# Tile-by-tile layer norms and moved products behind the experts of a two-block transformer kernel

## The reference, cut to what matters

```python
"""end of the first block: y is the experts' sum"""
x = layer_norm(ALPHA1 * x + g2 * y, post2_g, post2_b)
for i in range(2):                       # second_block
    if i == 0: mix = pool_mixer(x)       # window means per group, 4 products of 256x256, bias, scale
    else:      mix = gated_deltanet(x)   # z = x @ w_z; qkv = silu(conv4(x @ w_qkv)); ba; chunked delta rule;
                                         # o = rms(o) * norm_w * silu(z); o @ w_out
    x  = layer_norm(ALPHA2 * x + mix, ln_gain[i, 0], ln_bias[i, 0])
    ff = square(relu(x @ mlp_w1[i])) @ mlp_w2[i]                       # 1024 -> 4096 -> 1024
    pe = sigmoid(x @ ple_gate_w[i] + ple_gate_b[i]) * (p[i] @ ple_proj[i])
    x  = layer_norm(ALPHA2 * x + ff + pe, ln_gain[i, 1], ln_bias[i, 1])
```

## Time and profile before

| | us |
|---|---|
| three runs | 2159.33, 2158.49, 2153.45 (median 2158.49) |
| profiled execution, device time | 2157.81 |
| its span | 2156.1 |
| TensorE busy in the span | 1956.4 |
| experts (first to last of their products) | about 350 to 1390 |
| mean granted TensorE clock | 0.972 |

### The profile page before, as it was taken

How to read it: one execution, slowest core, us unless ns; L and a number is a source line. 1 busy time by engine, 2 the same in 40 slices (tenths; PEclk the granted TensorE clock), 3 DMA queues, 4 the chain that set the end, 5 groups by cost and what they waited for, 6 DMA issues and landing times. The chain is left out here.

```text
span 2156.1 us, 28523 instructions
## 1 busy us (share of the span) xinstructions
PE 1956.4 (91%) x10917; PEld 1229.7 (57%) x10918; DVE 914.4 (42%) x1463; ACT 456.6 (21%) x525; POOL 68.4 (3%) x123
## 2 busy tenths in 40 slices
PE   4999896999998989999988999779997898889997
PEld 2759764433333334333333343369986887868986
DVE  3799544111111111111111111366545887875554
ACT  2223101000000000000000000124532443324541
POOL 2000002000000000000000000000000000020000
PEclk9999997999999999999999999989999999999999
DMA  9694834959999999899999786464554420054551
GB/s 360 235 329 138 300 137 176 406 211 422 422 422 422 421 423 421 337 422 422 421 422 421 323 375 282 187 207 160 176 199 154 154 99 1 2 182 147 194 188 67
DMA packets 143588, 581.37 MB, mean 270 GB/s; under 512 B 10504, under 2 KB 12536, under 8 KB 94265
## 3 DMA queue, kind: packets, MB, share of 16 engines
q1 hardware_dynamic: 135824, 563.12, 67.1%
q0 software_dynamic: 3040, 11.02, 1.6%
q10 hardware_dynamic: 4649, 6.17, 0.8%
HBM read 579.23 MB, written 1.05 MB: 269 GB/s over the span
## 5 line engine op out<-in xcount | busy, mean ns | idle before, releaser
L1153 PE MATMUL bank<-ring,area 128*64 128x512 f32 x2048 | 461.4, 599 | 28.5 <-DMA ring<-in_w_gu 27.9
L1153 PEld LDWEIGHTS bank<-ring,area 128*64 128x64 f32 x2048 | 144.4, 137 | 327.6 <-issue 236.7
L895 PE MATMUL bank<-area_r,ring_r 128*128 128x256 f32 x992 | 284.6, 287 | 9.5 <-DVE area_r L2029 7.1
L897 PE MATMUL bank<-area_r,ring_r 128*128 128x256 f32 x992 | 282.9, 285 | 0.0
L898 PE MATMUL bank<-area_r,ring_r 128*128 128x256 f32 x992 | 282.8, 285 | 0.0
L288 DVE TENSOR_TENSOR ring_r<-ring,ring_r 128x2048 fp32r<-128x2048 f32 x90 | 206.1, 2292 | 176.6 <-ACT ring_r L285 176.1
L2297 DVE TENSOR_SCALAR area<-bank 128x512 f32<-128x512 f32 x36 | 24.9, 692 | 542.5 <-PE bank L1153 542.5
L285 ACT ACTIVATE ring_r<-ring 128x2048 fp32r<-128x2048 f32 x92 | 175.9, 1913 | 207.5 <-PE bank L898 188.8
L895 PEld LDWEIGHTS bank<-area_r,ring_r 128*128 128x128 f32 x992 | 192.8, 194 | 12.1 <-DVE area_r L2029 7.3
L1191 PE MATMUL bank<-area 128*64 128x512 f32 x864 | 192.5, 594 | 0.5 <-DVE area L2311 0.5
L897 PEld LDWEIGHTS bank<-area_r,ring_r 128*128 128x128 f32 x992 | 192.7, 194 | 0.5 <-issue 0.5
(11 more groups left out here) (331 smaller groups left out, 2048.5 us busy)
## 6 DMA issues: line engine op xcount, KB each, us to landing
ring<-in_w_gu SPq DMA_DIRECT2D x256, 1024.0 KB, 21.2
area<-in_w_dn SPq DMA_DIRECT2D x96, 1024.0 KB, 21.5
ring<-in_mlp_w SPq DMA_DIRECT2D x64, 1024.0 KB, 5.4
ring<-in_w_dn SPq DMA_DIRECT2D x32, 1024.0 KB, 19.9
ring<-in_w_in SPq DMA_DIRECT2D x24, 1024.0 KB, 6.2
ring<-in_gdn_w_in SPq DMA_DIRECT2D x16, 1024.0 KB, 5.5
area<-in_w_mod SPq DMA_DIRECT2D x12, 1024.0 KB, 8.8
ring<-in_w_mod SPq DMA_DIRECT2D x8, 1024.0 KB, 17.2
```

Source lines behind the costliest of these rows:

```text
L895: ins = mm(out_, a_[0], b_[0], start=start, stop=False)
L897: mm(out_, a_[0], b_[1], start=False, stop=False)
L1153: ins = mm(bk[hf * BLK:(hf + 1) * BLK, :], x(kt), block_u[:, c:c + BANK], start=False, stop=kt == ND - 1)
```

## The change

- **Norms by tile.** `layer_norm` behind the experts becomes `tile_norm(t)`; tile 0 is normalised, transposed (`tile_features`) and multiplied (`tile_part`) before tile 1. `tile_part` issues the eight products of a unit's slices with x's high part first and waits for the low part only then. Each part of the gate runs for three units on tile 0, then on tile 1, then unit 3 on both. `copy_high`, `x_low` and `residual` take a tile. The last quarter of w2 is ordered by tile. The last norm's tiles are written out one by one.
- **Projection moved.** `p @ ple_proj` and the transposes of p stand behind the experts and behind gdn_out (`p_product`); ScalarE keeps the result in SBUF (`ple`). Block 0's p and w_proj are loaded by SP before the late stream.
- **GpSimd** multiplies x by ALPHA1 during the experts, adds the experts' banks times g2, scales the pooling weights and bias, loads them earlier, gives one root per tile, and splits low parts of gate units 1 and 2 (both blocks) and of z0's second unit (`unit_low_here`).
- **z and silu.** z's first half goes ahead of qkv in the stream, in the groups and on TensorE; silu of slab s-1 goes ahead of the copies of slab s.

```diff
...
+                add_slab("z0", gdn_in, 3 * C)
                 add("qkv", slabs(gdn_in, range(0, 3 * C)))
-                add("z", slabs(gdn_in, range(3 * C, 4 * C)))
+                add_slab("z1", gdn_in, 3 * C + 1)
...
+        group("pT_0", 1)
+        group("proj_0", 4)
         group("pooled", 4)
         group("pool_tok", 4)
         for i in range(2):
             if i == 1:
                 group("x4T", 4)
+                group("z0", 2)
...
-                group("z0", 2)
...
+                group("pT_1", 1)
+                group("proj_1", 4)
             group(f"xT_{i}", 4)
-            group(f"pT_{i}", 1)
             group(f"gate_{i}", 4)
-            group(f"proj_{i}", 4)
...
+            sp.wait_ge(w_used, PRE + NU * (NE - 1))
+            sp.dma_start(p_tok[0], A["p_2"][0, 0].rearrange("(t p) c -> p t c", p=P)).then_inc(ple_in, 16)
+            sp.dma_start(ple_proj[0], A["ple_proj_2"][0].rearrange("(k p) n -> p k n", p=P)).then_inc(ple_in, 16)
             for n in range(PRE, len(stream)):
                 load(n)
-            sp.wait_ge(x_ready, 5 * NT)
-            sp.dma_start(out[0].rearrange("(t p) d -> p t d", p=P), x_tok).then_inc(out_done, 16)
-            sp.wait_ge(out_done, 16)
+            for t in range(NT):
+                sp.wait_ge(x_ready, 4 * NT + t + 1)
+                sp.dma_start(out[0, t * P:(t + 1) * P, :], x_tok[:, t, :]).then_inc(out_done, 16)
+            sp.wait_ge(out_done, 16 * NT)
...
+            pool.wait_ge(xn_ready, 3 * NT)
+            link(nc.gpsimd.tensor_scalar(x_tok, x_tok, ALPHA1, None, ALU.mult))
+
+            def tile_root(t):
+                inverse_root(rstd[:, t:t + 1])
+
+            def unit_low_here(i):
+                pool.wait_ge(w_high, i + 1)
+                pool.wait_ge(w_split, i)
+                nc.gpsimd.tensor_tensor(unit_low(i), ring[:, i % RING2, :, :], unit_high(i), ALU.subtract)\
+                    .then_inc(w_split, 1)
+
+            full(pool, G("moe", 3))
+            pw = a(6).rearrange("p (g k d) -> p g k d", g=4, k=2)
+            for dst, src in ((pool_b_bc, A["pool_b_2"][0].rearrange("(o g) d -> o (g d)", o=1).to_broadcast([P, D])),
+                             (pool_scale_bc, A["pool_scale_2"][0:1, :].to_broadcast([P, D])),
+                             (pw, A["pool_w_2"][0].rearrange("g (k p) d -> p g k d", p=P))):
+                pool.dma_start(dst, src).then_inc(pool_loads, 16)
+            ytmp = tok(4)
+            for t in range(NT):
+                for hf in range(NH):
+                    cs = slice(hf * BANK, (hf + 1) * BANK)
+                    emptied(pool, G("moe", 2 * t + hf))
+                    nc.gpsimd.tensor_tensor(x_tok[:, t, cs], x_tok[:, t, cs], ytmp[:, t, cs], ALU.add)\
+                        .then_inc(moe_added, 1)
+            tile_root(0)
+            pool.wait_ge(pool_loads, 48)
+            link(nc.gpsimd.tensor_tensor(pool_b_bc, pool_b_bc, pool_scale_bc, ALU.mult))
+            nc.gpsimd.sem_inc(scaled, 1)
+            tile_root(1)
+            for k in range(2):
+                nc.gpsimd.tensor_tensor(pw[:, :, k, :], pw[:, :, k, :], pool_scale_bc.rearrange("p (g d) -> p g d", g=4),
+                                        ALU.mult).then_inc(scaled, 1)
+            load_norm(3)
+            unit_low_here(LATE["gate0"] + 1)
+            tile_root(0)
+            unit_low_here(LATE["gate0"] + 2)
+            tile_root(1)
...
-            norm_root()

...
-            norm_root()
+            tile_root(0)
+            unit_low_here(LATE["z0"] + 1)
+            tile_root(1)
...
+                unit_low_here(LATE["gdn_out"] + i)
             inverse_root(s_["sso"][:, 1, :])
-            norm_root()
+            tile_root(0)
+            unit_low_here(LATE["gate1"] + 1)
+            unit_low_here(LATE["gate1"] + 2)
+            tile_root(1)
...
+            def p_product(i):
+
+                pe.wait_ge(ple_in, 32 * (i + 1))
+                transposed(G(f"pT_{i}"), [(p_tok[i][:, t, m * P:(m + 1) * P], m * S + t * P)
+                                          for m in range(2) for t in range(NT)])
+                emptied(pe, G(f"pT_{i}"))
+                pT = p_T[i].rearrange("p (m t) -> p m t", m=2)
+                for s in range(NH):
+                    for t in range(NT):
+                        g = G(f"proj_{i}", NT * s + t)
+                        claim(pe, g)
+                        for k in range(2):
+                            ins = mm(bank(g)[:, :], pT[:, k, t * P:(t + 1) * P],
+                                     ple_proj[i][:, k, s * BANK:(s + 1) * BANK], start=k == 0, stop=k == 1)
+                        fills(ins, g)
+
+            p_product(0)
...
-            for hf in range(NH):
-                for t in range(NT):
+            for t in range(NT):
+                for hf in range(NH):
...
+            def tile_features(gname, t, done):
+
+                pe.wait_ge(x_ready, done + t + 1)
+                for hf in range(NH):
+                    transposed(G(gname, NH * t + hf),
+                               [(x_tok[:, t, (4 * hf + m) * P:(4 * hf + m + 1) * P], m * P) for m in range(4)])
+
+            def tile_part(name, g, gname, highs, h, t):
+
+                u = late_unit(LATE[name] + h)
+                hf = h % 2
+                if hf == 0:
+                    claim(pe, g)
+                pe.wait_ge(x_high, highs + NH * t + hf + 1)
+                for k in range(UK):
+                    high = parts_of(xs, UK * hf + k, slice(t * P, (t + 1) * P))[0]
+                    for j in range(2):
+                        ins = mm(bank(g)[:, :], high, u[j][:, k, :], start=hf == 0 and k == 0 and j == 0, stop=False)
+                        settle(ins)
+                emptied(pe, G(gname, NH * t + hf))
+                for k in range(UK):
+                    low = parts_of(xs, UK * hf + k, slice(t * P, (t + 1) * P))[1]
+                    ins = mm(bank(g)[:, :], low, u[0][:, k, :], start=False, stop=hf == 1 and k == UK - 1)
+                if hf == 1:
+                    fills(ins, g)
+                    if t == NT - 1:
+                        owed[0] = True
+                elif t == NT - 1:
+                    ins.then_inc(w_used, 1)
+
             def ffn(i):
-                to_features(f"xT_{i}", x_tok, x_ready, NT * (1 + 2 * i))
...
+                def gate_part(n_unit, t):
+                    tile_part(f"gate{i}", G(f"gate_{i}", NT * (n_unit // 2) + t), f"xT_{i}", 12 * i, n_unit, t)
+
+                for t in range(NT):
+                    tile_features(f"xT_{i}", t, NT * (1 + 2 * i))
+                    for n_unit in range(SPLITS):
+                        gate_part(n_unit, t)
+                for t in range(NT):
+                    gate_part(SPLITS, t)
...
-                    for c in range(C):
+                    for c, t in (((0, 0), (0, 1), (1, 0), (1, 1)) if kq < KQ - 1 else ((0, 0), (1, 0), (0, 1), (1, 1))):
                         u = late_unit(n0 + C * kq + c)
...
+                        g = G(f"w2_{i}", NT * c + t)
...
                         if kq == KQ - 1:
-                            owed[0] = True
+                            fills(ins, g)
+                            owed[0] = t == NT - 1
+                        elif t == NT - 1:
+                            ins.then_inc(w_used, 1)
...
-            to_features("x4T", x_tok, x_ready, NT * 2)
-            for q in range(4):
-                emptied(pe, G("x4T", q))
+            for t in range(NT):
+                tile_features("x4T", t, NT * 2)
+                for h in range(2):
+                    tile_part("z0", G("z0", t), "x4T", 4, h, t)
...
-            for h in range(2):
-                z_half(0, h)
...
+            p_product(1)
...
+            p_columns(0)
             late.below(2)
+            p_products(0)
+            late.below(3)
...
+            def copy_high(gname, t):
+
+                for hf in range(NH):
...
+                    f(feat_r(X_HIGH)[:, 4 * hf:4 * hf + 4, t * P:(t + 1) * P],
+                      bank(g)[:, :].rearrange("p (m c) -> p m c", c=P), ACT.Copy).then_inc(x_high, 1)
...
+                late.below(w0 + 3)
+                for t in range(NT):
+                    copy_high(f"xT_{i}", t)
...
-            copy_high("x4T")
+            copy_high("x4T", 0)
+            late.below(LATE["qkv"] + 1)
+            copy_high("x4T", 1)
...
+            late.below(w0 + 3)
+            silu_z(0)
             for s in range(6):
                 late.below(w0 + 2 * s + 4)
-                if s >= 2:
-                    act.wait_ge(conv4_ready, s - 1)
+                if s:
+                    silu(s - 1)
...
-                if s:
-                    silu(s - 1)
-                late.below(w0 + 2 * s + 5)
+                if s < 5:
+                    late.below(w0 + 2 * s + 5)
             silu(5)
-            late.below(w0 + 16)
...
-            load_ffn(1)
```

(67 more changed lines are left out.)

167 lines of the change are left out of this document (61 added, 106 removed).

## The result

The changed kernel took 2135.6 us (median of four runs, 2132.9 to 2138.5) against 2156.2 for the kernel before beside it: ratio 0.990, 95% interval 0.988 to 0.992. Four further runs of it gave 0.988 (0.985 to 0.990). The forecast was 2117 us, with a range of 2104 to 2138: the direction and the range held, but the gain is 20.6 us where 41.5 were forecast. The profiled execution took 2138.45 us (span 2136.7), at the upper edge of the four.

A forecast was written before the change was run, and what follows sets the result against it. The prediction took TensorE, busy 91% of the span, as the bound, leaving its idle time, slow clock and the end to win. Its terms 20 + 20 + 1 + 4 - 3 = 42 took 2158.5 to about 2117 us, range 2104 to 2138.

The forecast's parts named there:

- A: From the experts' last product to w1 of block 0: earlier pooling and gate by tile save 20 us.
- The term for GpSimd beside VectorE, -3: Of 35 us new GpSimd work, some 4 lie beside VectorE passes of two SBUF tensors: 3 us lost, bounds 0 and -28.
- Rival 1: Contention in full: each VectorE pass under a long GpSimd instruction is held, norms late at A and B; 2141, chance 0.10.
- ALPHA1, costed at nothing: GpSimd's multiply of x by ALPHA1 has the whole expert loop to hide in: no cost.
- its own sign: Account of A is wrong if block 0's gate starts after 1424; its first product was forecast near 1418.
- B: From the end of block 0's w2 to the first k transposes: 123.8 us become 103.6, 20 saved, TensorE waiting 6.
- C: From gdn_out's end (F) to block 1's w1: queue order and banks collide, 5.9 us wait, gate at F+19.1; saves 1.
- Rival 2: No bank collision in C, or ScalarE passes pT sooner: gate at F+11.7, 8 us more, 2109; chance 0.12.
- D: The end: tile 0 finished and sent before products end, tile 1 done 4.6 us after them instead of 8.0; saves 4.
- Rivals 3 to 5: Qkv slabs VectorE-bound, 2127, chance 0.13; gate and z0 products at half clock, 2171, 0.03; edits ineffective, 2158, 0.02.

The follow-up runs named there:

- the run with all pieces: Changed kernel with GpSimd's long instructions cut to 512 columns, ALPHA1 multiply behind the routing, ScalarE's order and projection banks behind gdn_out changed: 2115.0 us, ratio 0.981.
- The bench: Changed kernel whole, with 27 pairs of GpSimd and VectorE operations timed beside each other on idle memory behind its end: 2221.6 us.

## Why the prediction was right and wrong

- **A, forecast 20, measured 6.5.** The adds were priced right (1.24 us each for 1.25), and the order of events is that of the text. The times were not. The gate starts 13 us later than forecast, counted from the experts' end. Along the path VectorE and GpSimd lose to each other 0.9 (first pass), 1.0 and 0.9 (roots, 1.56 and 1.47 for 0.56), 0.8 (the bias), 2.0 (tile 1's second pass), 3.0 (L2491) and 4.1 us (tile 0's second pass), together 12.7. They are not all on one path, and w1 starts 14.4 us later than forecast. Pieces win back 6.9. No run takes GpSimd out of A altogether: in the run with all pieces A is still 7.5 us over the forecast, and its stretched rows add up to some 6. So for that half the hold is read from rows and not shown by an edit.
- **The term for GpSimd beside VectorE, -3, is the step that failed.** "Some 4 us of it lies beside such passes": the sum counted how long the two overlap, where it had to count the rest of GpSimd's instruction at each pass that comes up under it. The 35 us were the right amount of work; in place of the 3, the rows show 12.7 (A), 4.1 (C) and 0 to 6 in the routing. Rival 1 had the mechanism and, at 2141, nearly the time. It was given 0.10, with L2521 counted for it and, against it, that reads with a PSUM side are not stretched and that most of the 35 us fall where VectorE has slack. The first of these is true and no argument, since the norm passes have no PSUM side; the second failed at the passes named above. L2521's 0.6 us are the same rule: it came up 0.7 us before the end of the splits. One row with a short overlap can't tell a hold from a proportion.
- The Trainium skill states the rule outright (SBUF — State Buffer, on the two sides of the memory): the pair of ports is an exclusive lock, taken for the whole instruction by whichever comes first, against VectorE instructions in a two-port mode or with two SBUF inputs, the latter only against a GpSimd instruction that reads SBUF. The bench agrees in all cases but one, the memset's too: beside the one-tensor multiply, operations of two tensors are let go 3.5 us after its start and not at its end at 5.36, and there the measurement decides. The forecast cited another page of it, which speaks of contention only, and weighed that as a rate.
- **ALPHA1, costed at nothing: wrong.** "The whole loop to hide in" asked whether GpSimd has time, not who is working when it starts. It cost about 3 us in the profile.
- **B, forecast 20, measured 19.7: right**, with its 6 us wait and the vanished ones. Its parts were off: the text gave z0 about 5 us for itself, where all but silu gives 12.3 alone and 9.1 on top of silu, and the new wait is partly slack. That the hold cost nothing here was luck: two passes missed GpSimd's split by a fraction of a us, and the forecast had not looked at that.
- **C, forecast 1, measured -3.5.** Collision, order, 5.9 us wait and the gate's start (F+19.6 for F+19.1) are confirmed to half a us once the hold is gone, and C then takes 43.0 for 43.6 before; the hold adds the rest. Rival 2 did not come, as the text had argued.
- **D, forecast 4, measured 4.0: right.** Rivals 3 to 5 did not come: the slabs run without waits at 12.4 us, the gate's stretch in A had a mean clock of 0.90 (its first products alone slow), and the gain is there.
- **The rest** is in front: 7.4 us. The routing alone took 7.5 longer, some 3 of them the hold and 4.6 the clock of the router.

The range held because it was drawn nearly to rival 1's 2141, not because the forecast was near. Half of the forecast gain is missing, and by its own sign (the gate's start) the account of A was wrong.

## What to carry to other kernels

Before giving elementwise work to GpSimd, list what VectorE does while it runs. Charge each elementwise operation that touches only SBUF with the rest of GpSimd's instruction, whatever its own length; operations with a PSUM operand and the norm's statistics went free here. Keep such instructions on GpSimd short (the bench's 512-column subtraction lets VectorE begin 1.1 us after its start) or start them where VectorE has long waits. With a queue order written by hand, ask of each new first item what stands behind it: two lines swapped on ScalarE and other banks for eight groups gave nearly 11 us here, 4 of them by taking a held pass off the path.
